# One gather of modulation rows moved behind the filters, a convolution cut into ten pieces, another order in attention, and two column chunks of the last product by seven half products

## The chip, the cores and the metric

The kernel runs on one core of one Trainium2 chip, as one program with hand-written instruction streams for five engines: TensorE (PE in the profile; PEld is its weight load), VectorE (DVE), ScalarE (ACT), GpSimd (POOL) and SyncE (SP, which issues most loads). All values are float32. The metric is the device time of one execution in microseconds, the median of several runs.

## What is computed

The reference is one inference step through two layers for 640 tokens of width 1024 (512 latent tokens of a request being denoised, 128 context tokens of a new one). The parts that the change touches:

```
for i in range(DEPTH):                                   # DEPTH = 2
    sh, sc, gt = adaln(cond, mod_w[i], mod_b[i])         # silu(cond) @ mod_w + mod_b, in three
    h = rms_norm(x, pre_norm_g[i]) * (1.0 + sc) + sh
    if i % 2 == 0:   y = even_mixer(h, ...)              # gated DeltaNet beside a Hyena long convolution
    else:            y = odd_mixer(h, ...)               # grouped-query attention beside latent attention
    x = x + gt * rms_norm(y, post_norm_g[i])

# even layer: filters of the long convolution from a small sine network; q, k, v by a depthwise
# convolution and SiLU; in chunks: sol = triangular_solve(I + strict(kb k^T * decay), rhs)
filt = hyena_filters(L, w1, b1, w2, b2, w3, sin_freq)
qkv = silu(depthwise_conv(concat([zq, zk, zv]), conv_w))

# odd layer
s = einsum('bqhgd,bkhd->bhgqk', q, k) * scale;  p = softmax(s);  o = einsum('bhgqk,bkhe->bqhge', p, v)
y = concat([o_g * silu(gg), o_m * silu(mg)]) @ out_w     # 640 x 1024 by 1024 x 1024
```

## The kernel before

TensorE is fed from the other engines through PSUM: eight banks of 128 x 512 values, used in rotation. The list `FILLS` numbers every filling of a bank in the order of the program; `bank(f)` is bank f mod 8, `full(f)` and `free(f)` are its semaphores, `wait_full`, `wait_drained` (the reader of f is done) and `wait_free` (the reader of f - 8 is done) are the waits on them. Each engine runs its own stream in the order in which the code stands, and waits at its head. Weights come in chunks of 1 MB (`chunk_list`, `load_chunk`) into three ring slots and some spare ones; SyncE issues them in order, each after the last reader of what the slot held. A float32 matmul shows as two instructions of TensorE in the trace, a transpose as one.

The stages on which the change bears, in order of time:

- **Start.** TensorE runs the sine network for the filters (`film`), transposes parameter vectors, gathers two chunks of the modulation matrix (`gather_modulation((0, 0))` and `((0, 1))`, 8 small matmuls each against its 1 MB chunk), repeats a product of ones (`keep_warm`, whose result nobody reads), then makes the filters of order 0 (`filt0`, ten products), transposes the first gathered rows (`turn_modulation`) and gathers `(0, 2)`.
- **Inverse of the chunks' triangular matrices** (`inv_groups`: group 0 has tiles 0 and 1, in two directions, so four chains). `invert_blocks` makes 16 x 16 inverses on VectorE; `turn4` transposes them; then `merge_level` doubles the block size three times (`LEVELS`). In a level TensorE multiplies a first round for the four chains (16 matmuls of 64 columns, `LT` by `Tinv`), VectorE scales the result (`scale_steps`), TensorE multiplies a second round (`Uinv` by the scaled `Xl`), VectorE adds it into `Tinv` (`add_steps`), and TensorE transposes it, ScalarE copying it to `Uinv`. Between these stand steps for group 1: `sum_decays(4)` (with `take_decays(4)` on ScalarE and masks on GpSimd), `key_products(t)` and its reader `take_keys(t)` on VectorE, and the value convolution `convolve_qkv(5, ...)`: two halves (`parts`) of five taps each over 128 x 644 values, SiLU behind it on ScalarE (`silu_rows`).
- **Attention** in ten units (`UNITS`; units 4 and 8 are of the context tokens). TensorE's loop over u: transposes of the probabilities of u (`turn_probabilities`, which ScalarE copies), scores of u + 2, values of u. VectorE's loop: `maxima(u + 2)`, `normalise(u + 2)` once ScalarE's exponentials are done, `gate_output(u)`, which multiplies the values with the gates into `mix` and frees their bank.
- **Output product** of the odd layer: `project_out(j, t)`, eight matmuls of 256 columns, for 4 column chunks j and 5 token tiles t, context tile first. ScalarE squares each tile for the norm (L1390), VectorE multiplies it with the gate (L2983); behind the last chunk GpSimd takes the root, and VectorE adds into x (L2988).

The odd layer's input product already uses a scheme of seven half products: `seven_products(s)` on TensorE with `half_product`, `sum_chunks`, `sum_rows` and `add_products` on VectorE, `copy_first` on ScalarE. For two column chunks side by side, tokens and weights are split into 2 x 2 blocks; sums of blocks are formed, seven products replace eight, and their results are added up again.

Of the kernel before, what the change touches and what calls it, by code (L numbers as in the profile page):

```python
# [23 lines left out]
P = 128  # L24
# [52 lines left out]
def scan_steps():  # L77

    fills = [("scan0.a", 2), ("scan0.b", 4)]
    for i in range(1, NT):  # L80
# [8 lines left out]
FILLS = [("film", 2), ("vectors", 2), ("film2", 2), row((0, 0)), row((0, 1)),  # L89
         ("filt0", 2 * NT), col((0, 0)), row((0, 2)), ("filt1", 2 * NT)] \  # L90
# [8 lines left out]
         ("keys2", 2), ("inv0", CHAINS[0]), ("sums4", 2), ("inv0_0", 3 * CHAINS[0]), ("keys3", 2),  # L99
# [10 lines left out]
         ("out1_0", 1), ("att_last", 1), ("out1", 4 * NT - 1)]  # L110
# [118 lines left out]
def program(nc, a, out, consts):  # L229
# [3 lines left out]
    with ctx:  # L233
# [125 lines left out]
        def spread(n, e):  # L359
# [26 lines left out]
        wsum_half = [[view(12928 + 2048 * s + 512 * n, 4, P) for n in range(4)] for s in range(2)]  # L386
        first, second, third = [view(27136 + 512 * n, 512) for n in range(3)]
# [84 lines left out]
        middle_ready = sem("middle_ready")  # L472
        oinv_ready = sem("oinv_ready")
# [19 lines left out]
                 [start["out1_0"]] + [start["out1"] + n for n in range(4 * NT - 1)]]  # L493
        in_f = {j: [start["in_tm0.3"] + n - 3 if j == 0 and n >= 3 else start["in_tm%d" % j] + n for n in range(NT)]
                for j in (0, 5)}
        st_f = [[start["st%d" % s] + n for n in range(8)] for s in range(6)]
# [35 lines left out]
        def chunk_halves(s):  # L532

            if s < 2:
# [27 lines left out]
        def chunk_list():  # L562
# [32 lines left out]
            for j in range(4):  # L595
                lst.append((a["odd_out_w"][0], WC * j, WC, out_f[1][NT * j + NT - 1]))
# [76 lines left out]
        def _(pool):  # L673
# [159 lines left out]
            for n in range(2 * KD):  # L833
                if n == KD:
# [3 lines left out]
                                        ALU.mult).then_inc(diag_ready, 1)  # L838
            for n, t in enumerate(OUT_ORDER):
                pool.wait_ge(ysum_ready, n + 1)  # L840
                inverse_roots(yst[:, 1, t:t + 1], yst[:, 0, t:t + 1], D, yrstd_ready)
# [3 lines left out]
        def _(act):  # L845
# [257 lines left out]
            for n, g in enumerate(inv_groups):  # L1103
# [5 lines left out]
                if n == 0:  # L1109
                    take_decays(4)  # L1110
                    silu_rows(v_cm, v_cm, 20)
# [5 lines left out]
                for l in range(len(LEVELS) - 1):  # L1117
                    for m, (t, d) in enumerate(chains):
                        f = g["levels"][l] + 2 * nch + m
                        wait_full(act, f)  # L1120
                        nc.scalar.activation(Uinv[:, 2 * t + d, :], bank(f), ACT.Copy).then_inc(free(f), 1)
                for m, (t, d) in enumerate(chains):
# [86 lines left out]
            def copy_first(s):  # L1209

                f, w = st_f[s][0], 512 if s < 2 else WC
# [172 lines left out]
            for j in range(4):  # L1384
                for n, t in enumerate(OUT_ORDER):
                    f = out_f[1][NT * j + n]
                    wait_full(act, f)
                    if (j, n) != (0, 0):
                        act.wait_ge(ypart_ready, NT * j + n)
                    nc.scalar.activation(sqs[:, 0:WC], bank(f)[:, 0:WC], ACT.Square,  # L1390
                                         accum_out=stat[:, 0, 4 * t + j:4 * t + j + 1]).then_inc(ypart_ready, 1)

# [1628 lines left out]
```

## Time and profile before

| what | us |
|---|---|
| median of 3 runs (lowest, highest) | 1008.84 (1008.42, 1009.04) |
| the profiled execution | 1007.34 |
| its span, to which all places in the trace refer | 1005.5 |
| TensorE busy | 984.0 (98%) |
| VectorE, ScalarE, GpSimd busy | 588.5, 298.5, 120.3 |
| mean granted clock of TensorE, share of full | 0.991 |

Times of single instructions and of waits come from the trace of the profiled execution, counted from the start of the span. The granted clock is given as a share of 2.4 GHz: 1.00 is 2.4 GHz and 0.50 is 1.2 GHz. An instruction at the lower clock lasts longer and counts as busy, so a slow clock doesn't show in the busy share.

### The profile page before, as it was taken

To read this page: it belongs to the slowest core of one execution; us is meant where nothing else is said; L and a number is where in the kernel's file an instruction comes from. 1 tells how busy PE (TensorE), PEld (TensorE's weight loads), DVE (VectorE), ACT (ScalarE), POOL (GpSimd) and SP (SyncE) were. 2 spreads that over 40 slices of the span, in tenths; PEclk is the share of its full clock that TensorE was granted. 3 is DMA by queue.
4 is the path that set the end of the run, shared out by engine and by line. 5 is a ranking of instruction groups with operands and counts; after the bars stand their busy time and mean duration, and the time that the engine had idled before them with its cause. 6 is when DMAs were issued, how large, how long until landed. Compare 5 with 4: busy or idle time off the path is not lost.

```text
span 1005.5 us, 13384 instructions
## 1 busy us (share of the span) xinstructions
PE 984.0 (98%) x5211; PEld 721.1 (72%) x5211; DVE 588.5 (59%) x1242; ACT 298.5 (30%) x780; POOL 120.3 (12%) x169
## 2 busy tenths in 40 slices
PE   6999999999999999999999999999999999999997
PEld 2447667554665566979999888888999755556786
DVE  3657555998965489885387233431757565453113
ACT  3053110201122345532202134114311565444111
POOL 4010000030300152100232110200000300010001
PEclk8999999999999999899999999999999999999999
DMA  8743441130220200112148204720502100000102
GB/s 257 275 133 119 140 154 44 40 84 0 68 78 34 84 1 1 42 44 63 43 142 277 86 1 126 233 74 0 168 4 81 57 1 1 0 2 1 42 1 105
DMA packets 68422, 78.10 MB, mean 78 GB/s; under 512 B 2700, under 2 KB 64135, under 8 KB 68360
## 3 DMA queue, kind: packets, MB, share of 16 engines
q1 hardware_dynamic: 64258, 68.96, 21.9%
q0 software_dynamic: 2432, 7.56, 2.3%
q8 instruction: 42, 0.69, 0.3%
q10 hardware_dynamic: 1669, 0.72, 0.3%
q14 instruction: 21, 0.16, 0.1%
HBM read 73.74 MB, written 3.51 MB: 77 GB/s over the span
## 4 chain that ended last, share of the span: by engine, by line
PE 93%; DVE 3%; DMA 2%; ACT 1%; SPq 1%; issue 0%; POOLq 0%; POOL 0%; DVEq 0%; ACTq 0%
PE ps L1398 83%; PE ps L1617 5%; PE ps L1428 2%; DMA wring<-in_mod_w 2%; PE ps L2017 1%; ACT phase L1331 1%; DVE phase L2326 1%; PE ps L1533 0%; PE ps L1438 0%; ACT phase L1334 0%; PE ps L1801 0%; DVE phase L2328 0%; DVE phase L2949 0%; SPq L631 0%; DVE wring L2555 0%
## 5 line engine op out<-in xcount | busy, mean ns | idle before, releaser
L1398 PE MATMUL ps<-hT,wring 128*128 128x128 f32 (+4 forms) x1088 | 261.7, 399 | 0.0
L1398 PEld LDWEIGHTS ps<-hT,wring 128*128 128x128 f32 x1088 | 162.5, 191 | 96.0 <-issue 89.6
L1398 PE MATMUL ps<-phase 128*128 128x256 f32 (+4 forms) x760 | 207.1, 420 | 3.7 <-DVE mix L2959 1.3
L1398 PEld LDWEIGHTS ps<-phase 128*128 128x128 f32 (+1 forms) x760 | 128.7, 191 | 71.4 <-issue 51.1
L1398 PE MATMUL ps<-wring,mix 128*128 128x256 f32 x560 | 122.1, 379 | 0.8 <-DVE mix L2957 0.8
L1398 PEld LDWEIGHTS ps<-wring,mix 128*128 128x128 f32 x560 | 105.9, 190 | 15.8 <-DVE mix L2957 1.6
L1398 PE MATMUL ps<-phase,hT 128*128 128x256 f32 (+3 forms) x336 | 78.8, 391 | 0.8 <-ACT phase L1376 0.8
L1398 PEld LDWEIGHTS ps<-phase,hT 128*128 128x128 f32 x336 | 60.5, 190 | 16.6 <-issue 11.4
L1398 PE MATMUL ps<-hT,phase 128*128 128x64 f32 (+4 forms) x276 | 55.8, 345 | 0.0
L1617 PE MATMUL ps<-ident,phase 128*128 128x128 f32 x400 | 50.0, 279 | 0.5 <-ACT phase L1334 0.4
L1617 PEld LDWEIGHTS ps<-ident,phase 128*128 128x128 f32 x400 | 46.4, 144 | 5.3 <-issue 4.0
L1398 PEld LDWEIGHTS ps<-hT,phase 128*128 128x128 f32 x276 | 40.4, 191 | 9.6 <-issue 6.0
L1398 PE MATMUL ps<-xreg,phase 128*128 128x128 f32 (+1 forms) x352 | 46.2, 291 | 0.0
L1398 PEld LDWEIGHTS ps<-xreg,phase 128*128 128x128 f32 x352 | 40.9, 192 | 5.2 <-issue 4.2
L2792 DVE TENSOR_TENSOR phase<-ps,phase 128x512 f32<-128x512 f32 (+1 forms) x26 | 14.5, 564 | 50.7 <-PE ps L1398 47.9
L2983 DVE TENSOR_TENSOR phase<-ps,phase 128x256 f32<-128x256 f32 x20 | 8.4, 421 | 43.4 <-ACT pad L1390 43.4
L1331 ACT ACTIVATE phase<-ps,nmax 128x512 f32<-128x512 f32 x32 | 22.1, 690 | 30.6 <-DVE nmax L2931 30.6
L2930 DVE TENSOR_REDUCE smax<-ps 128x1 f32<-128x512 f32 x32 | 21.9, 684 | 13.8 <-PE ps L2017 13.1
L1003 ACT ACTIVATE pad<-ps 128x512 f32<-128x512 f32 x16 | 9.4, 596 | 69.2 <-PE ps L1398 59.7
L2326 DVE SCALAR_TENSOR_TENSOR xreg<-pad,vec,xreg 128x644 f32<-128x644 f32 x32 | 28.5, 890 | 1.1
L729 POOL TENSOR_TENSOR phase<-xreg 128x1024 f32<-128x1024 f32 x2 | 6.8, 3385 | 182.7 <-DVE xreg L2449 182.7
L1398 PE MATMUL ps<-mix,phase 128*128 128x64 f32 (+1 forms) x104 | 26.7, 420 | 1.1 <-DVE mix L2616 1.1
(390 smaller groups left out, 1278.6 us busy)
## 6 DMA issues: line engine op xcount, KB each, us to landing
wring<-in_mod_w SPq DMA_DIRECT2D x18, 1024.0 KB, 5.2
wring<-in_even_in_w SPq DMA_DIRECT2D x16, 1024.0 KB, 5.8
phase<-in_mod_w SPq DMA_DIRECT2D x6, 1024.0 KB, 5.2
wring<-in_odd_in_w SPq DMA_DIRECT2D x5, 1024.0 KB, 9.0
phase<-in_odd_in_w SPq DMA_DIRECT2D x4, 1024.0 KB, 10.4
wring<-in_odd_out_w SPq DMA_DIRECT2D x4, 1024.0 KB, 5.3
wring<-in_even_out_w SPq DMA_DIRECT2D x3, 1024.0 KB, 10.2
xreg<-in_x_sample SPq DMA_DIRECT2D x1, 2048.0 KB, 16.9
```

The costliest lines, as they stand in the source:

```text
L729: chained(nc.gpsimd.tensor_tensor(U4, YQ[:, 0:2, :], YQ[:, 2:4, :], ALU.subtract))
L1003: nc.scalar.activation(pad[:, m, 2:2 + LS], bank(f + m), ACT.Copy).then_inc(free(f + m), 1)
L1331: nc.scalar.activation(prob[u % 2][:, g, 0:LS], bank(f + 1 + g), ACT.Exp, scale=scale, bias=nmax[:, u % 2, g:g + 1], accum_out=ssum[:, u % ...
L1398: return nc.tensor.matmul(o, l, r, start=first, stop=last)
L1428: ins = nc.tensor.matmul(bank(f)[q:q + 32, 0:WC], scond[:, k, :], wchunk(i)[:, k, :], start=k < 4, stop=k >= 4, tile_position=(0, q))
L1617: ins = nc.tensor.transpose(bank(f)[:, h * P:h * P + P], src(h), idn)
L2017: return nc.tensor.matmul(o, qpT[half, h - 4, toks(t)], kpT[half, keys], start=False, stop=True, tile_position=(half.start, 0))
L2326: chained(stt(o, src, w, o, ALU.mult, ALU.add))
L2792: ins = tt(dst, block_of(s, bank(f)), block_of(s, other), ALU.add)
L2930: chained(nc.vector.tensor_reduce(smax[:, u % 2, 0, g:g + 1], bank(f + 1 + g), AXX, ALU.max))
L2983: tt(y[:, t, quarter], bank(f)[:, 0:WC], gb_l[1][:, 0 if t < TS else 1, quarter], ALU.mult)\
```

## The change

Four edits, each to several engines' streams:

1. `gather_modulation((0, 1))` moves behind `filt0`, before the gather of `(0, 2)`.
2. In the first inversion: `scale_steps` of level 16 comes before the value convolution, and that is cut up: taps 0 and 1 of the first half, adds of chains 0 and 1, tap 2, adds of chains 2 and 3, the rest. `sum_decays(4)` moves from ahead of the first round to behind the transposes of level 16, `key_products` of tile 3 from there to between the rounds of level 32. On ScalarE `take_decays(4)` and the SiLU of the values move behind the copies of level 16.
3. In attention VectorE does `gate_output(u)` before `normalise(u + 2)`; on TensorE the transposes of the last unit come before the values of unit 8, and the first output tile behind the values of unit 9.
4. Column chunks 1 and 2 of the output product become a seventh pair of `seven_products` (`OUT_PAIR`), between the plain chunks 0 and 3. GpSimd forms the four weight sums (`out_wsum`, 128 x 1024 each), VectorE the four token sums (`out_mixed`); the results of the latent tiles go to `out_raw`, are squared from there by ScalarE and multiplied with the gates by VectorE (`gate_tiles`).

```
-FILLS = [("film", 2), ("vectors", 2), ("film2", 2), row((0, 0)), row((0, 1)),
-         ("filt0", 2 * NT), col((0, 0)), row((0, 2)), ("filt1", 2 * NT)] \
+FILLS = [("film", 2), ("vectors", 2), ("film2", 2), row((0, 0)),
+         ("filt0", 2 * NT), col((0, 0)), row((0, 1)), row((0, 2)), ("filt1", 2 * NT)] \
...
+            wait_full(pool, units[FIRST_LATENT - 1]["s"])
+            for f in st_f[OUT_PAIR][6:8]:
+                wait_chunk(pool, chunk_of[f])
+            nc.gpsimd.tensor_tensor(T3, B22, B12, ALU.subtract).then_inc(out_wsum_ready, 1)
+            nc.gpsimd.tensor_tensor(T1, B12, B11, ALU.subtract).then_inc(out_wsum_ready, 1)
+            pool.wait_ge(out_wsum_ready, 2)
+            nc.gpsimd.tensor_tensor(T2, B22, T1, ALU.subtract).then_inc(out_wsum_ready, 1)
+            pool.wait_ge(out_wsum_ready, 3)
+            nc.gpsimd.tensor_tensor(T4, B21, T2, ALU.subtract).then_inc(out_wsum_ready, 1)
...
             gather_modulation((0, 0))
-            gather_modulation((0, 1))
             keep_warm(start["filt0"], 2)
...
                 if o == 0:
                     turn_modulation((0, 0))
+                    gather_modulation((0, 1))
                     gather_modulation((0, 2))
...
             take_keys(GROUPS[1][0])
-            convolve_qkv(5, (0,))
             scale_steps(inv_groups[0], 0)
+            convolve_qkv(5, (0,), (0, 1))
+            add_steps(inv_groups[0], 0, (0, 1))
+            convolve_qkv(5, (0,), (2,))
+            add_steps(inv_groups[0], 0, (2, 3))
+            convolve_qkv(5, (0,), (3, 4))
             convolve_qkv(5, (1,))
-            add_steps(inv_groups[0], 0)
+            scale_steps(inv_groups[0], 1)
             take_keys(GROUPS[1][1])
-            merge_level(inv_groups[0], 1)
+            add_steps(inv_groups[0], 1)
...
             for u in range(len(UNITS)):
                 if u + 2 < len(UNITS):
                     maxima(u + 2)
+                gate_output(u)
+                if u + 2 < len(UNITS):
                     normalise(u + 2)
-                gate_output(u)
...
+            wait_drained(pe, units[-2]["p"])
+            project_out(0, TP, out_f[1][0])
             wait_drained(pe, units[-1]["p"])
-            for j in range(4):
-                for n, t in enumerate(OUT_ORDER):
-                    if (j, n) != (0, 0):
-                        project_out(j, t, out_f[1][NT * j + n])
+            for n, t in enumerate(OUT_ORDER[1:]):
+                project_out(0, t, out_f[1][n + 1])
+            seven_products(OUT_PAIR)
+            for n, t in enumerate(OUT_ORDER):
+                project_out(3, t, out_f[1][3 * NT + n])
```

The order on TensorE in the start, before: `wring,scond` are gathers, `one` the warm-up, `mix,phase` the filters, `ident` the transposes.

```order
L1428 MATMUL ps<-wring,scond 32x256 x16
L1398 MATMUL ps<-one 128x512 x2
L1398 MATMUL ps<-mix,phase 128x512 x10
L1438 MATMUL ps<-ident,pad 128x128 x2
L1428 MATMUL ps<-wring,scond 32x256 x8
L1398 MATMUL ps<-mix,phase 128x512 x10
```

The same place on TensorE after:

```order
L1471 MATMUL ps<-wring,scond 32x256 x8
L1441 MATMUL ps<-one 128x512 x2
L1441 MATMUL ps<-mix,phase 128x512 x10
L1481 MATMUL ps<-ident,pad 128x128 x2
L1471 MATMUL ps<-wring,scond 32x256 x16
L1441 MATMUL ps<-mix,phase 128x512 x10
```

Eight matmuls, one gather, have passed the warm-up, ten filter products and the transposes.

The order on VectorE from the keys of tile 2 to those of tile 3, before: `wring<-ps,phase` is `take_keys`, `mix<-ps,phase` the scaling, 128 x 644 the taps of the convolution, `phase<-phase,ps` the adds.

```order
L2563 TENSOR_TENSOR phase<-ps,phase 128x512 x2
L2322 TENSOR_SCALAR phase<-pad,vec 128x644
L2326 SCALAR_TENSOR_TENSOR phase<-pad,vec,phase 128x644 x3
L2328 SCALAR_TENSOR_TENSOR phase<-pad,vec,phase 128x644
L2616 SCALAR_TENSOR_TENSOR mix<-ps,phase 128x256 x4
L2322 TENSOR_SCALAR phase<-pad,vec 128x644
L2326 SCALAR_TENSOR_TENSOR phase<-pad,vec,phase 128x644 x3
L2328 SCALAR_TENSOR_TENSOR phase<-pad,vec,phase 128x644
L2628 TENSOR_TENSOR phase<-phase,ps 128x16x16 x4
L2555 SCALAR_TENSOR_TENSOR wring<-ps,phase 128x128 x8
```

The same place on VectorE after, as far as the second half of the convolution:

```order
L2616 TENSOR_TENSOR phase<-ps,phase 128x512 x2
L2669 SCALAR_TENSOR_TENSOR mix<-ps,phase 128x256 x4
L2375 TENSOR_SCALAR phase<-pad,vec 128x644
L2379 SCALAR_TENSOR_TENSOR phase<-pad,vec,phase 128x644
L2682 TENSOR_TENSOR phase<-phase,ps 128x16x16 x2
L2379 SCALAR_TENSOR_TENSOR phase<-pad,vec,phase 128x644
L2682 TENSOR_TENSOR phase<-phase,ps 128x16x16 x2
L2379 SCALAR_TENSOR_TENSOR phase<-pad,vec,phase 128x644
L2381 SCALAR_TENSOR_TENSOR phase<-pad,vec,phase 128x644
L2375 TENSOR_SCALAR phase<-pad,vec 128x644
L2379 SCALAR_TENSOR_TENSOR phase<-pad,vec,phase 128x644 x3
L2381 SCALAR_TENSOR_TENSOR phase<-pad,vec,phase 128x644
```

The four scalings now stand ahead of all ten taps, and the adds, in pairs, inside the first five.

The order on TensorE from the values of unit 7 on, before: `ident` the transposes of units 8 (4) and 9 (20), `phase,hT` the values (128 columns unit 8, 512 columns units 7 and 9), `wring,mix` plain output matmuls.

```order
L1398 MATMUL ps<-phase,hT 128x512 x5
L1617 MATMUL ps<-ident,phase 128x128 x4
L1398 MATMUL ps<-phase,hT 128x128 x4
L1617 MATMUL ps<-ident,phase 128x128 x20
L1398 MATMUL ps<-wring,mix 128x256 x8
L1398 MATMUL ps<-phase,hT 128x512 x5
L1398 MATMUL ps<-wring,mix 128x256 x152
```

The same place on TensorE after:

```order
L1441 MATMUL ps<-phase,hT 128x512 x5
L1660 MATMUL ps<-ident,phase 128x128 x24
L1441 MATMUL ps<-phase,hT 128x128 x4
L1441 MATMUL ps<-phase,hT 128x512 x5
L1441 MATMUL ps<-wring,mix 128x256 x48
L1441 MATMUL ps<-phase 128x256 x24
L1441 MATMUL ps<-wring,mix 128x256 x16
L1441 MATMUL ps<-phase,mix 128x256 x8
L1441 MATMUL ps<-wring,mix 128x256 x8
L1441 MATMUL ps<-wring,phase 128x256 x8
L1441 MATMUL ps<-wring,mix 128x256 x40
```

The 20 transposes of unit 9 follow those of unit 8 at once, the first output tile has moved behind the last values, and of 160 output matmuls of 256 columns 152 are left.

## Rows read from the trace of the kernel before

**Rows 1.** Waits of TensorE: waiting operation, releaser: us in total, times, longest.

```profile
PE ps L1428 <- DMA wring<-in_mod_w: 6.7, 2, 4.3
```

**Rows 2.** Timeline of the start: start us, us, engine line operation, [idle before, releaser].

```profile
17.99 1.93 PE L1428 MATMUL ps<-wring,scond 128*32 128x256 f32 x16 [2.46 <-DMA wring<-in_mod_w]
...
21.36 0.06 DVE L2204 MEMSET phase<- 64x1 f32 x1 [0.83 <-ACT phase L892]
...
24.21 1.94 PE L1428 MATMUL ps<-wring,scond 128*32 128x256 f32 x16 [4.29 <-DMA wring<-in_mod_w]
...
28.59 8.74 PE L1398 MATMUL ps<-mix,phase 128*128 128x512 f32 x20
...
37.48 1.07 PE L1428 MATMUL ps<-wring,scond 128*32 128x256 f32 x16
```

**Rows 3.** Short stretches: us, busy of five engines, granted clock, DMA share, GB/s.

```profile
17.20:17.40 0.20, 0.00 (x0) 0.00 (x0) 0.20 (x1) 0.00 (x0) 0.10 (x1) 0.61 1.08 343
...
27.40:27.60 0.20, 0.20 (x1) 0.03 (x1) 0.00 (x0) 0.00 (x0) 0.00 (x0) 0.79 1.08 343
...
413.10:413.20 0.10, 0.10 (x3) 0.10 (x3) 0.10 (x1) 0.10 (x2) 0.00 (x0) 0.95 0.00 0
...
420.00:420.10 0.10, 0.10 (x3) 0.10 (x2) 0.00 (x0) 0.10 (x1) 0.00 (x0) 0.91 0.00 0
```

**Rows 4.** Timeline of the first merge, TensorE and VectorE.

```profile
406.47 3.68 PE L1398 MATMUL ps<-phase,wring 128*128 128x64 f32 x32
...
409.07 1.81 DVE L2328 SCALAR_TENSOR_TENSOR phase<-pad,vec,phase 128x644 f32<-128x644 f32 x1
...
410.81 1.40 DVE L2616 SCALAR_TENSOR_TENSOR mix<-ps,phase 128x256 f32<-128x256 f32 x4
411.27 5.37 PE L1398 MATMUL ps<-mix,phase 128*128 128x64 f32 x32 [1.12 <-DVE mix L2616]
...
416.76 3.54 PE L1617 MATMUL ps<-ident,phase 128*128 128x128 f32 x16
...
420.13 1.95 PE L1398 MATMUL ps<-phase 128*128 128x128 f32 x16
421.22 2.16 DVE L2555 SCALAR_TENSOR_TENSOR wring<-ps,phase 128x128 f32<-128x128 f32 x8 [3.53 <-PE ps L1398]
...
423.49 1.29 DVE L2563 TENSOR_TENSOR phase<-ps,phase 128x512 f32<-128x512 f32 x2
...
425.44 3.74 PE L1398 MATMUL ps<-mix,phase 128*128 128x64 f32 x32
...
429.01 1.92 PE L1617 MATMUL ps<-ident,phase 128*128 128x128 f32 x16
```

**Rows 5.** Timeline of the last units of attention, TensorE, VectorE and ScalarE.

```profile
883.67 0.46 PE L1398 MATMUL ps<-phase 128*128 128x128 f32 x2 [1.31 <-DVE mix L2959]
...
918.89 0.16 DVE L2943 TENSOR_TENSOR ssum<-ssum 128x4 f32<-128x4 f32 x1 [1.36 <-ACT phase L1334]
...
919.30 1.94 DVE L2949 TENSOR_SCALAR phase<-phase,rsum 128x640 f32<-128x640 f32 x4
920.03 0.60 PE L1617 MATMUL ps<-ident,phase 128*128 128x128 f32 x4
...
921.15 0.68 DVE L2957 TENSOR_TENSOR mix<-ps,mix 128x512 f32<-128x512 f32 x1
...
922.38 2.35 PE L1617 MATMUL ps<-ident,phase 128*128 128x128 f32 x20
...
923.01 2.56 ACT L1376 ACTIVATE phase<-ps 128x512 f32<-128x512 f32 x5 [1.75 <-PE ps L1617]
...
928.02 4.46 PE L1398 MATMUL ps<-phase,hT 128*128 128x512 f32 x10
```

**Rows 6.** The chain that ended last (start, us, what), and the page's costliest groups.

```profile
933.25 65.89 PE ps L1398 x304
...
L729 POOL TENSOR_TENSOR phase<-xreg 128x1024 f32<-128x1024 f32 x2 | 6.8, 3385 | 182.7 <-DVE xreg L2449 182.7
```

More of the change, by code:

```diff
@@ L1791, in _ @@
                         ins.then_inc(full(fl + n), 1)
+                    if g is inv_groups[0] and l == 1:
+                        key_products(GROUPS[1][1])
                     if l == len(LEVELS) - 1:
@@ L2779, in result_block @@
             def result_block(s, r, half):
+                if s == OUT_PAIR:
+                    return out_raw[:, 2 * r:2 * r + 2, WC * half:WC * half + WC]
                 if s < 2:
@@ L2989, in _, with sum_outputs, gate_tiles @@
                             .then_inc(x_ready, 1)
+            def sum_outputs():
+                A11, A12, A21, A22 = [mix[:, 4 * k:4 * k + 4, WC * r:WC * r + WC] for r in range(2) for k in range(2)]
+                S1, S2, S3, S4 = out_mixed
+                wait_drained(dve, units[-1]["p"])
+                tt(S1, A21, A22, ALU.add).then_inc(out_mixed_ready, 1)
+                tt(S3, A11, A21, ALU.subtract).then_inc(out_mixed_ready, 1)
+                dve.wait_ge(out_mixed_ready, 1)
+                tt(S2, S1, A11, ALU.subtract).then_inc(out_mixed_ready, 1)
+                dve.wait_ge(out_mixed_ready, 3)
+                tt(S4, A12, S2, ALU.subtract).then_inc(out_mixed_ready, 1)
+            def gate_tiles(r):
+                for t in (2 * r, 2 * r + 1):
+                    tt(y[:, t, WC:3 * WC], out_raw[:, t, :], gb_l[1][:, 0, WC:3 * WC], ALU.mult).then_inc(gated_ready, 1)
+            X, W, V, Z, R, V2, X2, Z2 = st_f[OUT_PAIR]
+            sum_outputs()
+            gate_plain(0)
+            add_middle(OUT_PAIR)
+            dve.wait_ge(ypart_ready, NT + 2)
+            tt(y[:, TP, WC:3 * WC], bank(R), gb_l[1][:, 1, WC:3 * WC], ALU.mult).then_inc(free(R), 1)
+            add_third(OUT_PAIR)
+            wait_drained(dve, Z)
+            wait_drained(dve, V2)
+            gate_tiles(1)
+            add_last(OUT_PAIR)
+            wait_drained(dve, X2)
+            wait_drained(dve, Z2)
+            gate_tiles(0)
+            dve.wait_ge(gated_ready, TS)
+            wait_drained(dve, R)
+            gate_plain(3)
 _INS = ['x_prompt', 'x_sample', 'state_gdn_fwd', 'state_gdn_bwd', 'cache_gqa_k', 'cache_gqa_v', 'cache_mla_ckv',
```

118 lines of the change are left out of this document (77 added, 41 removed).

## The prediction

> **What bounds the kernel now.** I read the page first: TensorE is busy for nearly the whole span, so a microsecond can only go where TensorE has less to do, waits, or runs slow. Then the waits of TensorE: the longest entry is DMA, 6.7 us in two waits [rows 1], both in the first 25 us. Then, place by place, the timeline, and the granted clock in narrow stretches, since a slow clock counts as busy time. Four places come out, and the change touches each of them: the start [rows 2, 3], the first merge of the inversion [rows 3, 4], the end of attention [rows 5] and the last output product [rows 6]. The profiled execution took 1007.34 us, 1.84 more than its span; the median of the runs is 1008.84, 1.50 above it. I take both gaps as unchanged: what I subtract from the span I subtract from the median.
>
> **Start.** Before: the first gather of modulation rows ends at 17.99 + 1.93 = 19.92. TensorE then waits 4.29 us for the second chunk, gathers at the slow level (1.94 us against 1.07 later), runs two warm-up products, and starts the filters at 28.59; the third gather ends at 38.55 [rows 2]. After: warm-up, filters (8.74), two transposes (0.3, from the gap between the filters' end and 37.48), and two gathers of 1.07, all from 19.92 on. The second chunk is needed only some 12 us later, when it has long landed (24.21 before). The sine that the filters need is done at 21.4 [rows 2], inside the warm-up, so nothing new is waited for. What is open is the clock. It had fallen to half by 17.4 after the engine ran dry, and came back at 27.5, 3.3 us after dense work had begun at 24.21 [rows 3]. An instruction of a 512-wide product takes 8.74/20 = 0.43 us at 2.4 GHz, so the four of the warm-up take 3.4 us at 1.2 GHz: until 23.3, about 3.3 us after 19.92, and I let the filters run at the full clock from there. The third gather then ends at 23.3 + 8.7 + 0.3 + 2.1 = 34.4: **4.2 us gained**. Bounds: if the gather at 17.99 already counts as the dense work, the clock is back at 21.3, the warm-up ends 1.0 us sooner and the gain is 5.2; if it comes back only at 27.5 as before, 4.2 us of filters run at half speed and the gain is 2.1. SyncE's queue is passed too: the load into the second chunk's slot waits until about 33 instead of 26, and the loads behind it are queued. TensorE needs that load only after the second filters and several spectra, and x and the loads before it keep their places, so I cost it at nothing; if the cover failed it would be a DMA wait like the 4.29.
>
> **First merge.** Before, VectorE stands between TensorE's two product rounds of level 16: it does one whole half of the value convolution (its last tap took 1.81 us) before it scales the first round, so TensorE waits 1.12 us [rows 4]. Less than 2 us after it restarts, the clock falls to 1.2 GHz, at 413.2, and it stays there until 420.0 [rows 3]. The second round takes 5.37 us where the same 32 instructions take 3.74 one level later, and the 16 transposes 3.54 against 1.92 [rows 4]. Loss: 1.12 + 1.63 + 1.62 = 4.4 us. After, the scaling comes first, the convolution is cut up behind it, and the decay sums move from before the first round to after the transposes. I walk it from 404.7, where the decay sums began (1.8 us, as the keys' 16 instructions at 420.13 take up to 421.9): first round until 408.2; scaling (1.40 for four blocks) ends 0.2 + 0.35 after the last block, 408.8, while the first is ready at 406.2; second round 408.2 to 411.8; VectorE's adds, two taps and one tap apart, are done at 411.0 and 412.6, when the transposes, which start at 411.8, need them at 411.8 and 412.7. No wait is left. The rest of the convolution (0.9 a tap) ends near 418.6. Decay sums, the next first round and the keys of tile 3 fill TensorE until 420.6, and VectorE scales by 420.0. One new wait shows: the next second round writes the banks that hold the keys' products, and VectorE frees them only after 2.16 + 1.29 us of masking [rows 4], at about 423.5, when TensorE comes to the last bank at 423.3. I charge 0.3. ScalarE's sigmoid work and its table loads move behind the copies of level 16, and their readers come 5 us later or more. **4.1 us gained**; bounds 4.4 (no new wait) and 3.2 (the masking another 0.9 late, by what the tap of 1.81 us exceeded its usual 0.9 while GpSimd was at work).
>
> **Attention.** Two orders change. VectorE gates unit u before it normalises unit u+2. That takes away the 1.31 us for which the scores of unit 7 waited on a bank that the gating of unit 4 had to free, behind a normalisation [rows 5]: **1.3 gained**. But the gating waits for the values of its unit, so the last normalisation now starts late: values of unit 7 end at 920.03, gating 0.2 + 0.68, the two small operations and the scaling 919.30 - 918.89 + 1.94 = 2.35: ready at 923.3 instead of 921.24 [rows 5]. On TensorE the other change moves the transposes of the last unit ahead of the values of unit 8, so they are wanted at 920.5 already, and TensorE stands still for 2.8 us. From there: transposes at 923.3; copies done 923.01 + 2.56 - 922.38 = 3.2 later, 926.5, which also covers the values of unit 8; the last values 4.4, 930.9; the first output tile 3.5 (below), moved behind them, where it covers the last gating: 934.4. Before, the remaining tiles started at 933.25 [rows 5, 6]. **1.15 lost.** Then the clock. It fell after the standstill that ended the first film products (row at 17.2) and after the 1.12 us in the merge [rows 3, 4], but not after the 1.31 us at 882.4, so I expect it to fall after 2.8. It was low for 3.3 us of dense work in the start and for 6.85 us in the merge [rows 3]; half of that is lost, 1.65 to 3.4. What follows here is dense, so I take **2.0 lost**, near the lower end. The Trainium skill (TensorE: Matmul & The Clock Gate, section Why this matters for your kernels) warns only of idle gaps longer than this one; by it none of the 2.0 would be lost. The trace differs: in the merge the clock fell after a wait of 1.12 us [rows 3, 4].
>
> **Output.** 19 tiles of eight products took 65.89 us, 3.47 each [rows 6]. Of the two middle column chunks the four latent tiles cost 8 such units; seven half products of 8 matmuls cost 7, and the prompt tile's 2 stay. **3.5 gained.** The added work is hidden: four weight sums on GpSimd, 3.39 us each [rows 6], start after its diagonals near 884 and have over 50 us; four token sums on VectorE, even at GpSimd's price 13.6 us, run beside four tiles and the first half product (17.3 us). VectorE's additions of products and the gates are short against 3.47 us each, and the last of them stand behind the last half product with five plain tiles (17.3 us) still to come, so the tail after TensorE stays as it is. If the sums were late, TensorE would wait that long at the second half product.
>
> **Sum.** -4.2 - 4.1 - 1.3 + 1.15 + 2.0 - 3.5 = -9.95: 997.4 for a profiled execution, **998.8** for the median.
>
> **Rivals.**
> - The clock holds through the 2.8 us, as it did after 1.31: 2.0 less, 996.8. For it: all work around is dense, unlike the narrow products of the merge. Against it: the gap is twice as long. It is also what the rule of the Trainium skill named above gives.
> - The merge isn't cured: a wait or a fall of the clock stays there, since the narrow rounds now run one behind the other. Only the wait is gained, 1.1 instead of 4.1: 1001.8. Against it: the second level runs its two rounds back to back at the full clock [rows 4].
> - The start doesn't do what it says: the wait is only put off, because the late load of a later chunk is missed. Then its 4.2 are mostly given back: 1003.
> - Slower: the clock falls at the 2.8 us gap and stays at 1.2 GHz in the 66 us output stage, which now begins with it. Half of the low time is lost. The other terms and the lost 1.15 leave 11.95 us to use up, so it needs some 24 us of low clock, and 28 to be slower by over 0.2%. The longest low stretch seen is 10 us (17.3 to 27.5), and that one had 4.29 us of idling in it. Through the whole stage it would cost 31 us: 1028.
>
> **How the numbers follow.** Forecast 0.52; clock holds 0.22; merge not cured 0.13; start given back 0.08; slower 0.03; the rest, 0.02, lies beside these, near no change. The best bounds together (5.2, 4.4, no fall of the clock) give -13.3, 995.5; the worst of the forecast (2.1, 3.2, fall at 3.4) -5.6, 1003.3, but both worst ends together are unlikely, so I take 995.3 to 1002.3, which holds the forecast, the first two rivals and part of their spread. About 0.2% (2 us) is what a measurement of this kernel tells from no change. Faster by more: 0.94; within: 0.03; slower: 0.03.
>
> **What would show it.** No DMA wait of TensorE after 18 us, and the filters starting near 23. In the merge, no wait of TensorE between the rounds, a clock of 1.00 throughout, 3.7 us a round. No wait on the prompt unit's gating; instead one of nearly 3 us ahead of the last transposes, with the clock at 0.5 some time after it. Seven half products and the prompt's two tiles in 31 us (9 x 3.47), without a wait. The forecast is wrong by most if that gap is absent, if its low clock lasts, or if the clock falls in the merge all the same.

## The result, and the profile after

The changed kernel takes 994.92 us (median of 993.64, 994.92 and 995.22) against 1008.84: a ratio of 0.9863, 95% interval 0.9847 to 0.988, or 13.9 us less. The forecast was 998.8, with a range that began at 995.3; the direction was right, and the gain was 3.9 us larger than forecast. The profiled execution took 993.64 us with a span of 991.8, 13.7 less than the span before.

The waits of TensorE after (operation, releaser: us in total, times, longest), to be held against [rows 1]:

```profile
PE ps L1660 <- DVE phase L3009: 2.6, 1, 2.6
PE ps L1471 <- DMA wring<-in_mod_w: 2.5, 1, 2.5
```

One of the two DMA waits is gone; the wait on scaling in the merge and the wait at the scores of unit 7 are gone; a new one of 2.6 us on the normalisation (L3009) leads the list, and a small one of 0.2 us on the keys' masking (L2616) has come. All of these the prediction named.

The start, TensorE alone (start us, us, engine, line, operation, [idle before, releaser]), and the granted clock there (us, busy, clock, DMA share, GB/s):

```profile
4.59 2.50 PE L1441 MATMUL ps<-phase 33*128 33x512 f32 x4
...
18.08 1.07 PE L1471 MATMUL ps<-wring,scond 128*32 128x256 f32 x16 [2.54 <-DMA wring<-in_mod_w]
19.08 1.99 PE L1441 MATMUL ps<-one 128*128 128x512 f32 x4
21.51 8.85 PE L1441 MATMUL ps<-mix,phase 128*128 128x512 f32 x20 [0.44 <-DVE phase L2258]
...
30.50 1.93 PE L1471 MATMUL ps<-wring,scond 128*32 128x256 f32 x32
32.37 7.99 PE L1441 MATMUL ps<-mix,phase 128*128 128x512 f32 x18
```

```profile
17.00:18.00 1.00, 0.00 (x0) 1.00 1.11 350
18.00:19.00 1.00, 0.92 (x16) 1.00 1.10 347
```

In this execution the granted clock never fell in the start, where it was at half from 17.3 to 27.5 before [rows 3]. So the gather takes 1.07 us instead of 1.93, the two warm-up products 1.99, and the filters begin as soon as the sine is ready. The second filters begin at 32.37 instead of 38.48 (the third gather of [rows 2] starts at 37.48 and takes 1.07): 6.1 us gained in this pair of executions.

The first merge, TensorE, to be held against [rows 4]:

```profile
402.09 3.74 PE L1441 MATMUL ps<-mix,phase 128*128 128x64 f32 x32
405.66 1.92 PE L1660 MATMUL ps<-ident,phase 128*128 128x128 f32 x16
...
417.57 1.08 PE L1441 MATMUL ps<-mix,phase 128*128 128x64 f32 x8 [0.22 <-DVE phase L2616]
```

The second round now takes 3.74 us instead of 5.37, the transposes 1.92 instead of 3.54, and nothing is waited for between them; the granted clock is 1.00 in every stretch from 394 to 422. From the keys of tile 2 to the next projection it is 34.28 us, against 38.69 before: 4.4 gained.

The end of attention, and the clock there, to be held against [rows 5]:

```profile
907.77 0.60 PE L1660 MATMUL ps<-ident,phase 128*128 128x128 f32 x4
910.98 3.83 PE L1660 MATMUL ps<-ident,phase 128*128 128x128 f32 x20 [2.61 <-DVE phase L3009]
...
920.00 20.88 PE L1441 MATMUL ps<-wring,mix 128*128 128x256 f32 x96
```

```profile
910.00:911.00 1.00, 0.02 (x1) 0.77 0.00 0
...
912.00:913.00 1.00, 1.00 (x7) 0.50 0.00 0
...
914.00:915.00 1.00, 1.00 (x12) 1.00 0.00 0
```

TensorE stands still for 2.61 us, the clock falls near 910.5, and the last 20 transposes take 3.83 us instead of 2.35. The output stage then runs from 920.00 to the end of the chain without a wait:

```profile
914.80 70.99 PE ps L1441 x322
```

To compare the tails I use one interval throughout: from the transposes of unit 8 (907.77 here, 920.03 before) to the start of the output product, without the first output tile that before does in between (3.47 us). Before it is 933.25 - 3.47 - 920.03 = 9.75, here 920.00 - 907.77 = 12.23.

### The profile page after: what moved, and what is told of

The parts are those of the page before. It is cut to its first block, busy times and chain, and to the rows that moved or that the text cites. A ratio compares the mean times of both kernels' runs of the same rounds, so it can differ in the third digit from the quotient of the medians.

```text
span 991.8 us, 13358 instructions
## 1 busy us (share of the span) xinstructions
PE 976.9 (98%) x5195; PEld 716.1 (72%) x5195; DVE 596.0 (60%) x1248; ACT 299.9 (30%) x781; POOL 130.2 (13%) x173
## 4 chain that ended last, share of the span: by engine, by line
PE 95%; DVE 2%; ACT 2%; issue 0%; POOLq 0%; POOL 0%; DVEq 0%; ACTq 0%
PE ps L1441 85%; PE ps L1660 5%; PE ps L1471 2%; PE ps L2067 1%; ACT phase L1353 1%; PE ps L1576 0%; PE ps L1481 0%; ACT phase L1356 0%; PE ps L1844 0%; DVE wring L2608 0%; PE ps L1683 0%; DVE smax L2990 0%; DVE phase L3009 0%; DVE phase L2250 0%; DVE phase L2254 0%
## 5 line engine op out<-in xcount | busy, mean ns | idle before, releaser
L1441 PE MATMUL ps<-phase 128*128 128x256 f32 (+4 forms) x808 | 217.6, 418 | 1.6 <-DVE phase L2534 0.8
L1441 PEld LDWEIGHTS ps<-phase 128*128 128x128 f32 (+1 forms) x808 | 137.8, 191 | 70.4 <-issue 49.6
L1441 PE MATMUL ps<-wring,mix 128*128 128x256 f32 x464 | 101.6, 379 | 0.0
L1441 PEld LDWEIGHTS ps<-wring,mix 128*128 128x128 f32 x464 | 87.8, 190 | 12.2 <-issue 0.5
L2852 DVE TENSOR_TENSOR phase<-ps,phase 128x512 f32<-128x512 f32 (+1 forms) x33 | 19.3, 592 | 68.2 <-PE ps L1441 65.3
L1353 ACT ACTIVATE phase<-ps,nmax 128x512 f32<-128x512 f32 x32 | 22.1, 691 | 28.8 <-DVE nmax L2991 28.8
L1398 ACT ACTIVATE phase<-ps 128x512 f32<-128x512 f32 x42 | 21.9, 610 | 15.6 <-PE ps L1660 15.6
L1441 PE MATMUL ps<-phase,wring 128*128 128x64 f32 (+2 forms) x152 | 26.0, 323 | 0.0
```

The lines of the kernel that those rows point to most:

```text
L1353: nc.scalar.activation(prob[u % 2][:, g, 0:LS], bank(f + 1 + g), ACT.Exp, scale=scale, bias=nmax[:, u % 2, g:g + 1], accum_out=ssum[:, u % ...
L1398: nc.scalar.activation(probT[u % 2][:, k, :], bank(f), ACT.Copy).then_inc(free(f), 1)
L1441: return nc.tensor.matmul(o, l, r, start=first, stop=last)
L2852: ins = tt(dst, block_of(s, bank(f)), block_of(s, other), ALU.add)
```

## The experiments

Each ran against the kernel before on the same chip, in five rounds; that kernel's medians were 1008.48, 1008.70 and 1008.77 in the three series. The profiled executions of one kernel differ by a microsecond or more, so below a term is read from a stretch of the trace, and the median stands beside it. Where a ratio to the kernel before is given, the microseconds saved or lost are worked out from that ratio; the plain difference of the two medians lies up to 0.7 us beside it.

**The four edits one by one.** e1_start is the change's lines in the start and nothing else:

```
             gather_modulation((0, 0))
-            gather_modulation((0, 1))
...
                     turn_modulation((0, 0))
+                    gather_modulation((0, 1))
```

> The kernel before with the change's start alone: the second gather of modulation rows stands behind the first filters, nothing else is touched. Theory (clock): what the start is worth hangs on whether TensorE's clock falls near 17 us, while TensorE waits for the first chunk. Where it falls (as in the profiled execution of before) I expect about 4.2 us less, second filters near 34.3; where it holds (as in the profiled execution of after) 6.1 us less, second filters at 32.4. Executions should then come in two groups some 1.5 us apart, the longer ones with a mean clock about 0.005 lower. Rival (no clock): the prediction undervalued the removed wait itself; then every execution gains 6 us, with the clock low at 18 to 22 us or not.

Measured: 1003.17 us, ratio 0.9948 (0.9935 to 0.9961), 5.2 us less.

```profile
18.06 1.94 PE L1428 MATMUL ps<-wring,scond 128*32 128x256 f32 x16 [1.21 <-DMA wring<-in_mod_w]
19.92 3.02 PE L1398 MATMUL ps<-one 128*128 128x512 f32 x4
22.79 8.74 PE L1398 MATMUL ps<-mix,phase 128*128 128x512 f32 x20
...
33.54 7.99 PE L1398 MATMUL ps<-mix,phase 128*128 128x512 f32 x18
```

The clock was low in this execution from before 12 us until 22.1, inside the warm-up. The filters began at 22.8 and the second filters at 33.54, between the 32.4 and the 34.3 of the two cases, so the rival (6 us in every execution, whatever the clock) is out. That the longer executions would have the lower mean clock was wrong: here 1002.2 and 1002.5 us went with 0.990, 1003.2 to 1003.5 with 0.992. Here 1.2 us of the low clock fell into the wait for the first chunk, where it costs nothing; what counts is when the clock comes back.

e2_merge is the reordering of the first merge alone, on all engines:

```
-            convolve_qkv(5, (0,))
             scale_steps(inv_groups[0], 0)
+            convolve_qkv(5, (0,), (0, 1))
+            add_steps(inv_groups[0], 0, (0, 1))
...
```

> The kernel before with the change's first merge alone: scaling ahead of the value convolution, the convolution cut up between the additions, decay sums behind the first level's transposes, ScalarE's work moved with it. Theory: 4.1 to 4.4 us less (1.12 of wait, 1.63 and 1.62 of slow clock), no wait of TensorE between the rounds, clock 1.00 from 405 to 425, a wait of about 0.2 us for the keys' masking. Rival (only the wait is cured): 1.1 us less, with the clock low somewhere between 405 and 425.

Measured: 1003.64 us, ratio 0.9955 (0.9943 to 0.9967), 4.5 us less. The stretch from the keys to the projection is 34.28 us, as in the changed kernel, and the clock is 1.00 throughout it. The rival, that only the wait goes, is out.

e3_attention is the three orders in attention alone, with the plain output product; VectorE's lines of it:

```
...
+                gate_output(u)
+                if u + 2 < len(UNITS):
                     normalise(u + 2)
-                gate_output(u)
...
```

> The kernel before with the change's orders in attention alone: gating ahead of the normalisation, the last unit's transposes ahead of the prompt unit's values, the first output tile behind the last values; the output product stays eight plain products. By the prediction's terms: 1.31 us gained at the scores of unit 7, 1.15 lost by a standstill of 2.8 us ahead of the last transposes, 2.0 lost by the clock: 1.85 us longer, 0.15 shorter if the clock holds. By the trace of after, where the slow stretch was 3.1 us: about 1 us longer. Rival (the orders are a gain as a whole): 1 us shorter or more, no wait before the last transposes.

Measured: 1009.88 us, ratio 1.0012 (1.0002 to 1.0022): by itself this edit makes the kernel 1.2 us longer, with an interval from 0.2 to 2.2. The standstill is there, and in this execution the clock fell. By the rows of this study the edit makes 1.2 to 1.4 us longer where the clock falls and 0.1 shorter where it holds (1.31 gained at the scores of unit 7; in the tail 1.22 lost without a fall and 1.26 to 1.5 more with one, by the intervals here and in f1_after_again), so the median speaks for a fall in most of its executions. The uncured merge of the same execution shows how much the loss there varies, to be held against [rows 4]:

```profile
412.79 7.09 PE L1398 MATMUL ps<-mix,phase 128*128 128x64 f32 x32 [1.14 <-DVE mix L2618]
419.67 3.50 PE L1617 MATMUL ps<-ident,phase 128*128 128x128 f32 x16
...
921.37 0.60 PE L1617 MATMUL ps<-ident,phase 128*128 128x128 f32 x4
924.57 4.07 PE L1617 MATMUL ps<-ident,phase 128*128 128x128 f32 x20 [2.60 <-DVE phase L2951]
...
933.83 69.23 PE L1398 MATMUL ps<-wring,mix 128*128 128x256 f32 x320
```

The tail interval is 933.83 - 921.37 = 12.46. In the merge the slow clock lasted through the whole second round: keys to projection took 40.08 us, a loss of 5.8 where the profile of before had 4.4.

e4_output is the seven half products alone, with attention's orders as before:

```
-            for j in range(4):
-                for n, t in enumerate(OUT_ORDER):
...
+            seven_products(OUT_PAIR)
```

> The kernel before with the change's output product alone: the two middle column chunks of the four latent tiles by seven half products, orders in attention as before. Theory: one unit of eight products less, 3.5 us shorter (eight of 3.47 replaced by seven), TensorE without a wait from the second half product on. Rival (the sums are late): TensorE waits at the second half product, since the first output tile now runs ahead of the last values and only three tiles stand between the last gating and the half products; gain below 2.5 us.

Measured: 1004.01 us, ratio 0.9962 (0.9948 to 0.9976), 3.8 us less.

```profile
932.68 17.53 PE L1441 MATMUL ps<-wring,mix 128*128 128x256 f32 x80 [0.79 <-DVE mix L3008]
950.05 10.52 PE L1441 MATMUL ps<-phase 128*128 128x256 f32 x48
...
977.68 17.43 PE L1441 MATMUL ps<-wring,mix 128*128 128x256 f32 x80
```

The stage takes 62.43 us instead of 65.89 [rows 6]: one unit, 3.46. No wait stands ahead of the half products. Another 0.35 us comes from behind TensorE's end, where the span now ends 6.0 us later instead of 6.35, in every profile with the new output product. It lies behind the last operation of VectorE, which ends 3.4 us before the span does in the kernel before and 3.0 us before it in the changed one.

The four medians together make 5.2 + 4.5 - 1.2 + 3.8 = 12.3 us, where the whole change makes 13.8 in the same comparison; with some 1.0 to 1.4 us of uncertainty on each, the 1.5 between them is no larger than what the medians leave open.

**What the clock does in the start, and in the standstill.** f1_after_again is the changed kernel once more:

> The changed kernel itself, timed again. Theory: its executions differ by what TensorE's clock does before 22 us. Where it never falls there, the second filters start near 32.4 and the mean clock is about 0.997 (the profiled execution of after); where it falls, they start 1.0 to 1.9 us later and the mean clock is about 0.992. So 993.5 to 995.5 us, the lower clock going with the longer times. Rival: the spread is in the landing of the first chunks; then time and clock don't go together.

Measured: 994.99 us, ratio 0.9863 (0.9848 to 0.9878).

```profile
4.24 1.34 PE L1441 MATMUL ps<-phase 33*128 33x512 f32 x4
...
12.28 0.40 PE L1512 MATMUL ps<-ident,phase 99*128 99x99 f32 x1 [3.91 <-issue]
...
18.45 1.93 PE L1471 MATMUL ps<-wring,scond 128*32 128x256 f32 x16 [1.43 <-DMA wring<-in_mod_w]
20.32 3.78 PE L1441 MATMUL ps<-one 128*128 128x512 f32 x4
23.89 8.96 PE L1441 MATMUL ps<-mix,phase 128*128 128x512 f32 x20
...
34.87 5.42 PE L1441 MATMUL ps<-mix,phase 128*128 128x512 f32 x12
...
910.26 0.60 PE L1660 MATMUL ps<-ident,phase 128*128 128x128 f32 x4
913.47 2.40 PE L1660 MATMUL ps<-ident,phase 128*128 128x128 f32 x20 [2.60 <-DVE phase L3009]
...
921.23 4.05 PE L1441 MATMUL ps<-wring,mix 128*128 128x256 f32 x18
```

```profile
10.00:12.00 2.00, 0.00 (x0) 0.67 1.04 257
...
24.00:26.00 2.00, 2.00 (x6) 0.92 1.09 336
```

The same program, and both places come out the other way. In the start the clock fell near 10.7, in a wait of 3.9 us ahead of the transposes at 12.28, and came back at 24.3: the second filters begin at 34.87, 2.5 us later than in the first execution, more than the 1.9 that I had allowed. The rival, the landing of the first chunk, explains little of it: the first gather starts at 18.45 instead of 18.08.

Which way the start goes shows before 9 us. Where the four film instructions at 4.2 to 4.6 us take 1.34 to 1.52 us (e1, e2, f1, f3, f4, g2), the warm-up behind them is done by 9, TensorE waits 3.1 to 3.9 us ahead of the transposes at 12, and the clock falls between 10.7 and 11.8. Where they take 2.50 (before, the first execution of the changed kernel, e3, e4, f2, g3), that wait is 1.2 us or less, and the clock falls between 16.7 and 17.2, in the wait for the first chunk, or not at all. The granted clock reads 1.00 during the film in both groups, so only the durations tell them apart.

In the tail TensorE stood still for the same 2.60 us, and the clock held: the transposes take 2.40, the tail interval is 921.23 - 910.26 = 10.97, 1.26 less. Of the five profiled executions with this standstill the clock fell in two (the first one and e3_attention) and held in three (this one, f3_start_warm and g3_uncut).

f2_tail takes back VectorE's new order for the last normalisation alone:

```
+                if u + 2 == len(UNITS) - 1:
+                    normalise(u + 2)
                 gate_output(u)
-                if u + 2 < len(UNITS):
+                if u + 2 < len(UNITS) - 1:
                     normalise(u + 2)
```

> The changed kernel, but the last normalisation (unit 9) stands ahead of the gating of unit 7 again; all earlier units keep the new order, so the 1.31 us at the scores of unit 7 stay gained. Theory (the standstill makes the clock fall): the scaled rows are ready 1.28 us after the values of unit 7 end instead of 3.2, the standstill ahead of the last transposes shrinks from 2.6 to about 0.7 us, the clock holds, the transposes take 2.35 instead of 3.83: about 3.4 us less than the changed kernel. If the clock falls after 0.7 us too: 2 us less. Rival (the normalisation isn't what it waits for): no gain, the wait goes to the copies or the scores.

Measured: 992.06 us, ratio 0.9834 (0.9819 to 0.9849), 2.9 us less than the changed kernel beside it. TensorE and VectorE at this place:

```profile
909.98 0.60 PE L1660 MATMUL ps<-ident,phase 128*128 128x128 f32 x4
911.25 2.40 PE L1660 MATMUL ps<-ident,phase 128*128 128x128 f32 x20 [0.67 <-DVE phase L3009]
...
919.00 6.21 PE L1441 MATMUL ps<-wring,mix 128*128 128x256 f32 x28
```

```profile
909.25 1.94 DVE L3009 TENSOR_SCALAR phase<-phase,rsum 128x640 f32<-128x640 f32 x4
911.11 0.68 DVE L3017 TENSOR_TENSOR mix<-ps,mix 128x512 f32<-128x512 f32 x1
```

The scaling is done before the gating of unit 7, the standstill is 0.67 us, the clock holds, and the tail interval is 919.00 - 909.98 = 9.02: 1.95 less than where the clock held through the long standstill, 3.2 less than where it fell. The median's 2.9 lies between the two, nearer the second. The gain of 1.31 us at the scores of unit 7 stays; only this one use of the new order cost something.

f3_start_warm puts three more warm-up products where the changed kernel waits for the first chunk, and f4_both adds the mended tail to that:

```
+            keep_warm(start["filt0"], 3)
             gather_modulation((0, 0))
```

> The changed kernel with three more warm-up products between the last film product and the first gather, where TensorE waits 2.5 us for the first chunk. Theory (the clock sets the start): the clock no longer falls near 17, executions gather at the fast group: 0.5 to 1.5 us less at the median than the changed kernel, mean clock 0.996 or more in all. Where the clock had already fallen before 12 us the products run slowly and the gather is up to 1.3 us late, hidden by the sine at 21.5. Rival (the landing of the chunk and the sine set the start): nothing changes, within 0.3 us.

> The changed kernel with both edits: the last normalisation ahead of the gating of unit 7, and three more warm-up products ahead of the first gather. If the two are independent, their gains add: 3.4 and 0.5 to 1.5 us, some 990 to 991.5 us.

Measured: 995.33 us (0.9863, 0.9846 to 0.9879) and 992.58 us (0.9837, 0.982 to 0.9854): no gain from the products in either, and in f3_start_warm a mean clock of 0.993 to 0.997 where 0.996 or more was expected.

```profile
16.93 5.01 PE L1441 MATMUL ps<-one 128*128 128x512 f32 x6
21.87 1.07 PE L1471 MATMUL ps<-wring,scond 128*32 128x256 f32 x16
```

In this execution of f3_start_warm the clock had already fallen near 11, so the three products took 5.0 us and held the gather back until 21.87, which undid what a sooner return of the clock (21.3) gave; the second filters began at 35.45. An execution of f4_both in which the mean clock was 0.999 took 990.57, the others 992.0 to 993.7. What is left is the earlier wait, ahead of the transposes at 12 us. g1_warm_both fills that as well:

```
-            keep_warm(start["vectors"], 3)
+            keep_warm(start["vectors"], 5)
```

> The kernel with the last normalisation ahead of the gating of unit 7 and the three warm-up products ahead of the first gather, and two more warm-up products ahead of the two transposes at 12 us, where TensorE waited 3.1 to 3.9 us in the executions in which the clock had fallen by 11 us. Theory (that early wait decides the clock): the wait shrinks to about 2 us, the clock holds through the start in most executions, the second filters begin near 32.4 and the time is 990.5 to 991.5 us with a mean clock of 0.998. Rival (a wait of about 2 us makes it fall too): the executions spread as before, 990.5 to 993.7.

Measured: **990.84 us**, ratio 0.9822 (0.9808 to 0.9837), the lowest median of the study (its interval overlaps those of f2_tail and f4_both), with a mean clock of 0.997 or 0.998 in all four executions.

```profile
12.09 0.28 PE L1512 MATMUL ps<-ident,phase 99*128 99x99 f32 x1 [1.80 <-issue]
...
14.54 2.85 PE L1441 MATMUL ps<-one 128*128 128x512 f32 x6
...
31.55 8.85 PE L1441 MATMUL ps<-mix,phase 128*128 128x512 f32 x20
```

With the early wait down to 1.8 us and the next one filled, the clock stays at 1.00 through the start, and the second filters begin at 31.55, although the film took 1.34 us, as in the executions in which the clock fell near 11. The two early products alone, without the three ahead of the first gather, were not tried. Put together, the start of the profiled executions reads:

| kernel | granted clock low after 10 us | second filters begin |
|---|---|---|
| before; e4; e2; e3 | until 27.5; 27.0; 28.4; 30.4 | 38.48; 37.77; 39.16; 39.98 |
| g1_warm_both | never | 31.55 |
| the changed kernel, first execution | never | 32.37 |
| e1_start; g2_transposes | until 22.1; 21.7 | 33.54; 33.60 |
| g3_uncut; f2_tail; f1_after_again | until 23.7; 24.0; 24.3 | 34.38; 34.58; 34.87 |

The later the clock is back, the later the filters are done, with one pair out of order by 0.06 us. Without the change's edit the mean of the four is 38.85, with it (the six without added products) 33.89: 5.0 us.

**Two halves of an edit.** g2_transposes takes back the new order of TensorE's transposes alone, so that unit 8's values stand ahead of the last ones; the first output tile stays where the change put it:

```
-                if u < len(UNITS) - 1:
-                    turn_probabilities(u)
-                if u == len(UNITS) - 2:
-                    turn_probabilities(u + 1)
+                turn_probabilities(u)
```

> The changed kernel with one thing taken back on TensorE: the last unit's transposes stand behind the values of unit 8 again; VectorE's new order stays. The scaled rows are ready no sooner, so the last transposes start where they do in the changed kernel, 3.2 us after the values of unit 7; but the standstill is cut into two short ones, 0.8 us for the copies of unit 8's transposes and about 1 us for the scaled rows. Theory (the clock fell because of the one long standstill): the clock holds, the transposes take 2.35 instead of 3.83; the last values now wait some 1.0 us for the copies that unit 8's values covered: from 0.5 us less to 0.1 more than the changed kernel. If the clock falls all the same: 0.5 to 1 us longer than the changed kernel.

Measured: 993.66 us, ratio 0.9856 (0.9839 to 0.9872).

```profile
909.00 0.60 PE L1660 MATMUL ps<-ident,phase 128*128 128x128 f32 x4
910.38 1.13 PE L1441 MATMUL ps<-phase,hT 128*128 128x128 f32 x8 [0.78 <-ACT phase L1398]
912.21 2.40 PE L1660 MATMUL ps<-ident,phase 128*128 128x128 f32 x20 [0.70 <-DVE phase L3006]
915.60 4.53 PE L1441 MATMUL ps<-phase,hT 128*128 128x512 f32 x10 [0.99 <-ACT phase L1398]
919.96 5.34 PE L1441 MATMUL ps<-wring,mix 128*128 128x256 f32 x24
```

Three short waits instead of one long one, the clock holds, and the interval is 919.96 - 909.00 = 10.96. That is the 10.97 of f1_after_again, where the clock held through the long standstill too: in these two traces the order of the transposes is worth nothing by itself, and the 1.2 us between the two spans lie in the start (33.60 against 34.87). The median is 1.3 us below that of f1_after_again (0.7 by the ratios), where 0.5 was expected at most. Whether that is the start too, or short waits that keep the clock up more often than the long one, this run can't say.

g3_uncut leaves the first half of the value convolution in one piece:

```
-            convolve_qkv(5, (0,), (0, 1))
-            add_steps(inv_groups[0], 0, (0, 1))
...
+            convolve_qkv(5, (0,))
+            add_steps(inv_groups[0], 0)
```

> The changed kernel with the first half of the value convolution in one piece between VectorE's scaling and its additions in the first merge, instead of cut around the additions. Theory (cutting is needed): the second round still follows without a wait, but the additions come only when five taps are done, 4.0 us after the scaling: the transposes, which could start 3.1 us after the scaling's end, wait about 1.4 us, and with the clock falling once more the kernel is 1.4 to 4.5 us longer than the changed one. Rival (moving the scaling alone does it): no wait, same time as the changed kernel within 0.3 us.

Measured: 996.93 us, ratio 0.9884 (0.9867 to 0.99), 1.9 us longer than the changed kernel in f1_after_again.

```profile
404.09 3.74 PE L1441 MATMUL ps<-mix,phase 128*128 128x64 f32 x32
409.26 3.61 PE L1660 MATMUL ps<-ident,phase 128*128 128x128 f32 x16 [1.44 <-DVE phase L2682]
```

The second round follows without a wait, but the transposes wait 1.44 us for the additions, and the clock falls once more (3.61 instead of 1.92). So the convolution has to be cut. Keys to projection is 37.59 us in this execution, 3.3 more than in the changed kernel; two of the other three took 995.2 and 996.0 us, and whether the clock fell in them no trace shows. That the scaling stands first takes away the wait ahead of the second round; the move of the decay sums was not tried by itself.

## Why the prediction was too small, step by step

- **The clock in the tail, 2.0 us: the step that failed.** The prediction took what the clock does after a wait as fixed, from the one trace of before. Its sum charged a fall after the 2.8 us gap in full, at 2.0 us. The standstill came (2.6), but the clock fell in two of five traced executions, and where it fell it cost 1.26 (12.23 against 10.97) to 1.5. So the term was too large either way: by 0.5 to 0.74 us with a fall, by all of it without. How often it falls beyond the traces stays open: e3_attention's median, and f2_tail's 2.9 us where 1.95 goes with a held clock and 3.2 with a fall, speak for a fall in most executions. "The clock holds", the rival at 996.8, came true in three traces of five and deserved more than its chance of 0.22. The rule of the Trainium skill (TensorE: Matmul & The Clock Gate, section Why this matters for your kernels) warns only of longer idle gaps than this one. It gives the right result for three of these executions and the wrong one for the other two. In the merge the clock fell after a wait of 1.1 us in all four profiled executions without that edit (before, e1, e3, e4), and after 1.44 us in g3_uncut.
- **The start, 4.2 us: mis-sized, by the same step.** It measured 5.0 between the means of the table, and 6.1 between the two profiled executions first compared. The forecast took the clock to be back at 23.3 and the third gather to end at 34.4, against a start before whose second filters begin at 38.48. Where the clock did fall at 17 (f2, g3) that walk was close: back at 23.7 and 24.0, second filters at 34.38 and 34.58. But in other executions of the same start it fell earlier (back at 21.7 to 24.3) or never; the mean of the starts after is 33.89, about 0.4 us sooner than forecast, and that of the starts before 38.85, 0.4 us later than the one in the profile.
- **Profile and median.** "I take both gaps as unchanged" was nearly right: the median lies 1.50 us above the profiled execution before and 1.28 after. The miss is in the profiled execution itself, forecast at 997.4 and measured at 993.64, 3.8 us less. Of that the start makes 1.9, the clock in the tail, which did fall there, 0.74, the stretch behind TensorE's end 0.35, the merge 0.3; some 0.4 lies between the projection and the transposes of unit 8, where 1.73 us were gained and 1.31 forecast.
- **Merge, 4.1 us: right.** 4.4 in the trace, with the keys' wait at 0.22 where 0.3 was charged; 4.5 in the median. A loss of up to 5.8 before had not been foreseen.
- **Attention, 1.31 gained and 1.15 lost: right.** The scores of unit 7 no longer wait, and the tail interval grew by 10.97 - 9.75 = 1.22 without the clock.
- **Output, 3.5 us: right.** 3.46, with nothing late; the prediction held that the tail after TensorE stays as it is; 0.35 us of it went, and why was not tried.
- **Rivals.** No merge left uncured, no start given back: no chunk was late, and no DMA wait of TensorE follows after the first gather. The low clock in the output stage, which was to make the kernel slower, was over before the output product began, in both executions that had it (by 914 of 920.00, and by 928.1 of 933.83).

The prediction's own sum, 1008.84 - 9.95, is 998.9, where it wrote 998.8. With the start at 5.0 (0.8), the merge at 4.4 (0.3) and the stretch behind TensorE (0.35) it becomes 997.4; with the clock in the tail as measured, 996.7 to 996.9 where it falls and 995.4 where it holds. The measured 994.92 and 994.99 are nearer the second, while e3_attention and f2_tail speak for the first. The 0.5 us that remain in the second case are inside what the interval of the main comparison leaves open (1.7 to either side), the 1.8 to 2.0 in the first just outside.

## What to carry to other kernels

An order that frees one bank early can make the last user late: apply it to the units that wait, not to all. A term that hangs on the clock should be taken from several executions, as a share of them that pay and a price, and not from the one in the profile. Before a wait is filled with idle products, look for an earlier one that already lets the clock fall: the three products ahead of the first gather gained nothing alone (995.33 against 994.99), in a trace where the clock had fallen before they began, and with two more in the earlier wait the clock held.

## What the runs showed of the hardware

- The same standstill of 2.60 us, ahead of the same instructions, let TensorE's clock fall to 1.2 GHz in two executions and not in three; a wait of 1.1 us among 64-column products in the merge was followed by a fall in all four profiled executions that had it.
- The clock came back while TensorE ran only transposes: in the tail of the first execution it was at 1.00 by 914, and the transposes ran from 910.98 to 914.8; in e3_attention it was back at 928.1, in transposes that began at 924.57.
- The mean granted clock of a span is no measure of its time: e1_start's executions at 0.990 were 0.7 to 1.3 us shorter than those at 0.992. In the one of them that was traced, at 0.990, the clock was low from 11.8 to 22.1, in part while TensorE waited; the others have no trace.
